# One core, two layers with 16 experts: weights rotate through eight places, four experts a loop round

## What is computed

```python
aff = softmax(h @ w_router)                 # (tokens, 16)
gsel, idx = top_k(aff.T, C)                 # every expert picks C tokens: 64 latent and 16 context
xs = h[idx]                                 # (16, C, 1024)
hid = silu(xs @ w_gate[e]) * (xs @ w_up[e]) # 1024 x 1024 weights, one set for each expert
ye = (hid @ w_down[e]) * gsel
x = x + g2 * scatter_add(ye, idx)
```

## Time and profile before

| what | value |
|---|---|
| device time, median of 3 runs | 1809.16 us (1808.12 to 1811.6) |
| span of the profiled execution | 1807.7 us |
| PE busy | 1619.1 us (90%) |
| DVE, ACT, POOL busy | 829.0, 572.2, 391.3 us |
| DMA traffic | 502.59 MB, mean 278 GB/s |
| expert stages | about 420 to 900 us and 1302 to 1782 us |

### The profile page before, as it was taken

The page is one execution under the profiler, slowest core; times in us unless marked ns, Lnnn a source line. Parts: engine busy times, 40 slices in busy tenths (PEclk is TensorE's granted clock), DMA queues, the critical chain, the costliest instruction groups (busy, mean ns, idle before and its releaser), DMA issues. The chain is left out here.

```text
span 1807.7 us, 69734 instructions
## 1 busy us (share of the span) xinstructions
PE 1619.1 (90%) x27905; PEld 1281.1 (71%) x27905; DVE 829.0 (46%) x2593; ACT 572.2 (32%) x2228; POOL 391.3 (22%) x2166
## 2 busy tenths in 40 slices
PE   6999988986999999888869999899599998998885
PEld 3554457446999989888735554664389988998885
DVE  2299768262333323232245996943623232423233
ACT  2200245235545432211130003542355554221211
POOL 1100000002343424332310000000124333333332
PEclk9999999997999999999989999999799999999998
DMA  9356640237999999999953412221599999999992
GB/s 348 129 184 235 233 174 1 105 127 284 402 409 409 409 409 409 409 409 409 361 206 140 157 58 102 108 94 35 202 374 409 409 409 409 408 409 409 409 407 111
DMA packets 146722, 502.59 MB, mean 278 GB/s; under 512 B 6217, under 2 KB 6642, under 8 KB 146578
## 3 DMA queue, kind: packets, MB, share of 16 engines
q1 hardware_dynamic: 142288, 488.96, 69.5%
q0 software_dynamic: 3264, 10.88, 1.8%
q10 hardware_dynamic: 1026, 1.25, 0.2%
HBM read 494.76 MB, written 6.31 MB: 277 GB/s over the span
## 5 line engine op out<-in xcount | busy, mean ns | idle before, releaser
L950 PE MATMUL ps<-v_sb,weight_ring 128*64 128x80 f32 x16384 | 589.3, 234 | 51.7 <-DMA weight_ring<-in_w_gate_dram 20.8
L950 PEld LDWEIGHTS ps<-v_sb,weight_ring 128*64 128x64 f32 x16384 | 577.3, 138 | 63.0 <-DMA weight_ring<-in_w_gate_dram 25.0
L967 PE MATMUL ps<-v_sb,weight_ring 128*64 128x80 f32 x8192 | 296.7, 234 | 31.7 <-DVE v_sb L1693 19.9
L967 PEld LDWEIGHTS ps<-v_sb,weight_ring 128*64 128x64 f32 x8192 | 288.4, 138 | 40.0 <-DVE v_sb L1693 25.0
L705 PE MATMUL ps<-mix,weight_ring 128*128 128x128 f32 (+1 forms) x976 | 271.0, 439 | 2.1 <-ACT mix L1054 1.2
L1238 ACT ACTIVATE v_sb<-mix 128x8 f32 x1520 | 185.5, 205 | 223.6 <-PE ps L950 146.1
L1719 DVE TENSOR_TENSOR qk<-qk,v_sb 128x8 f32 x1520 | 212.3, 194 | 90.8 <-issue 90.0
L1848 POOL COPY v_sb<-mix 128x8 f32 x1040 | 145.2, 198 | 479.0 <-PE ps L950 417.7
L1861 POOL TENSOR_TENSOR qk<-qk,v_sb 128x8 f32 x1040 | 198.7, 232 | 181.7 <-DVE v_sb L1708 178.5
L705 PEld LDWEIGHTS ps<-mix,weight_ring 128*128 128x128 f32 x976 | 148.1, 194 | 122.8 <-issue 119.8
L1443 DVE SCALAR_TENSOR_TENSOR weight_ring<-u_gate,conv_cols,weight_ring 128x655 f32<-128x655 f32 x240 | 195.3, 899 | 0.0
(11 more groups left out here) (195 smaller groups left out, 1240.5 us busy)
## 6 DMA issues: line engine op xcount, KB each, us to landing
weight_ring<-in_w_down_dram SPq DMA_DIRECT2D x64, 2048.0 KB, 23.7
weight_ring<-in_w_gate_dram SPq DMA_DIRECT2D x48, 2048.0 KB, 20.9
weight_ring<-in_w_up_dram SPq DMA_DIRECT2D x48, 2048.0 KB, 23.6
weight_ring<-in_w_mod_dram SPq DMA_DIRECT2D x24, 2048.0 KB, 9.0
weight_ring<-in_w_in_dram SPq DMA_DIRECT2D x10, 2048.0 KB, 8.3
spare<-in_w_gate_dram SPq DMA_DIRECT2D x32, 512.0 KB, 10.4
weight_ring<-in_w_out_dram SPq DMA_DIRECT2D x4, 2048.0 KB, 9.4
rope_sb<-in_w_gate_dram SPq DMA_DIRECT2D x16, 512.0 KB, 11.3
```

What stands on the lines that cost most here:

```text
L950: last = nc.tensor.matmul(ps[c * HALF:(c + 1) * HALF, 2 * (i % 2) + f // BLK, f % BLK * CAP:(f % BLK + 1) * CAP], w[:, kk, o:o + HALF], pi ...
L967: last = nc.tensor.matmul(ps[c * HALF:(c + 1) * HALF, 4 + d // BLK, d % BLK * CAP:(d % BLK + 1) * CAP], w[:, kk, o:o + HALF], hid[:, k, :] ...
```

## The change

Units are numbered n = 0 to 95 over a layer, and unit n lies in place n mod 8. Places 0 to 5 are the ring, places 6 and 7 the eight pieces that were the relays, now called `annex`; TensorE reads its weights there directly, and ScalarE's copies are gone. As 8 places and 6 units an expert repeat after 24 units, TensorE's loop has four experts a round and four rounds. The row of the final norm goes to `past_k_t` and is loaded in layer 1's attention. The index registers of the adds are read ahead of the wait for the result: the first group of each expert, all groups of the last. Core of the diff:

```diff
+UNITS = 6
+PIECES = KD // 2
+PLACES = SLOTS + 2
+ROUND = 4
...
+        def unit_rows(l, q, j):
+            if q < SLOTS:
+                return ring[:, UNIT_SLOTS[l][q], j * D:(j + 1) * D]
+            return annex[q - SLOTS][j]
+
+        def freed(slot):
+            return UNITS * EXPERTS - PLACES + UNIT_SLOTS[0].index(slot) + 1
...
+            def expert_unit(l, n):
+                src, q = expert_src(l, n // UNITS, n % UNITS), n % PLACES
+                if q < SLOTS:
+                    sp.dma_start(ring[:, UNIT_SLOTS[l][q], :]..., src).then_inc(expert_loaded[q].sem, 16)
+                    return
+                for j in range(PIECES):
+                    sp.dma_start(annex[q - SLOTS][j], src[:, j, :]).then_inc(expert_loaded[q].sem, 16)
...
-                        sp.wait_ge(*expert_used.at(l - 1, 6 * (EXPERTS - 1) + i + 1))
+                        sp.wait_ge(*expert_used.at(l - 1, freed(PROJ_SLOTS[l][i])))
...
-                for u in range(2, first if l > 0 else 0):
-                    sp.wait_ge(*expert_used.at(l - 1, 6 * (EXPERTS - 1) + 3 + u))
+                for u in range(first if l > 0 else 0):
+                    sp.wait_ge(*expert_used.at(l - 1, freed(mod_slot(l, u))))
                     mod_unit(l, u)
...
-                for e in range(1, EXPERTS):
-                    refill_relays(e + 1)
-                    for i in range(RELAYS if e < RELAY_END else 0, 6):
-                        sp.wait_ge(*expert_used.at(l, e * 6 + (i - 5)))
-                        expert_unit(l, e, i)
+                for n in range(PLACES, UNITS * EXPERTS):
+                    sp.wait_ge(*expert_used.at(l, n - PLACES + 1))
+                    expert_unit(l, n)
...
-                with nc.Fori(0, EXPERTS, engines=[mybir.EngineType.PE], hint_back_edge=True) as e:
-                    gate_up(e)
-                    pe.wait_ge(*result_taken.at(l, e + 1))
-                    down(e)
+                with nc.Fori(0, EXPERTS // ROUND, engines=[mybir.EngineType.PE], hint_back_edge=True) as g:
+                    for j in range(ROUND):
+                        gate_up(g, j)
+                        down(g, j)
...
-                    if e + 1 < RELAY_END:
-                        for r in range(RELAYS):
-                            relay_copy(e + 1, r)
...
+                    starts = range(0, add_split(e), PICK_LOAD)
+                    ahead = len(starts) if e + 1 == EXPERTS else 1
+                    loaded = [picks_of(mybir.EngineType.Pool, e, at, PICK_LOAD) for at in starts[:ahead]]
+                    pool.wait_ge(*result_taken.at(l, e + 2))
...
-                    pool.wait_ge(*expert_loaded[0].at(l - 1, RELAY_END))
+                    pool.wait_ge(*expert_used.at(l - 1, UNITS * EXPERTS))
...
+                if l + 1 == DEPTH:
+                    pool.wait_ge(*scores_done.at(l, ATT))
+                    pool.dma_start(final_gain, final_norm_g...).then_inc(gain_loaded.sem, 16)
...
-            pool.wait_ge(*expert_loaded[1].at(DEPTH - 1, RELAY_END))
-            pool.dma_start(x_norm[:], final_norm_g...).then_inc(gain_loaded.sem, 16)
```

More of the change, by code:

```diff
@@ L218, in build @@
         out_loaded = [signal(f"out_loaded{b}", 1, 16) for b in range(2)]
-        expert_loaded = [signal(f"expert_loaded{i}", EXPERTS, 16) for i in range(6)]
+        expert_loaded = [signal(f"expert_loaded{q}", UNITS * EXPERTS // PLACES, 16 if q < SLOTS else 16 * PIECES)
+                         for q in range(PLACES)]
         expert_used = signal("expert_used", 6 * EXPERTS)
-        relay_loaded = [signal(f"relay_loaded{r}", RELAY * (RELAY_END - 1), 16) for r in range(RELAYS)]
-        relay_copied = [signal(f"relay_copied{r}", (RELAY - 1) * (RELAY_END - 1)) for r in range(RELAYS)]
         rope_loaded = signal("rope_loaded", unit=16)
@@ L445, in _ @@
                 first, units = MOD_EARLY[l], len(MOD_LIST[l])
-                for u in range(2):
-                    if l > 0:
-                        sp.wait_ge(*expert_used.at(l - 1, 6 * (EXPERTS - 1) + 3 + u))
+                for u in range(2 if l == 0 else 0):
                     mod_unit(l, u)
@@ L495, in _ @@
                         sp.wait_ge(*out_done.at(l, TILES))
-                    expert_unit(l, 0, i)
-                for r in range(RELAYS):
-                    if r == 1:
+                    expert_unit(l, i)
+                for n in range(SLOTS, PLACES):
+                    if n == SLOTS + 1:
                         sp.wait_ge(*x2_ready.at(l, TILES))
@@ L502, in _ @@
                         sp.wait_ge(*x2_transposed.at(l, TILES - 1))
-                    for j in range(RELAY):
-                        relay_piece(l, 1, r, j)
+                    expert_unit(l, n)
                 sp.wait_ge(*top_round.at(l, TOP_ROUNDS))
@@ L1712, in add_hi @@
                 def add_hi(e):
-                    for at in range(add_split(e), CAP, PICK_LOAD):
-                        rows = picks_of(mybir.EngineType.DVE, e, at, PICK_LOAD)
-                        if at == add_split(e):
-                            dve.wait_ge(*result_taken.at(l, e + 2))
+                    starts = range(add_split(e), CAP, PICK_LOAD)
+                    ahead = len(starts) if e + 1 == EXPERTS else 1
+                    loaded = [picks_of(mybir.EngineType.DVE, e, at, PICK_LOAD) for at in starts[:ahead]]
+                    dve.wait_ge(*result_taken.at(l, e + 2))
+                    for g, at in enumerate(starts):
+                        rows = loaded[g] if g < ahead else picks_of(mybir.EngineType.DVE, e, at, PICK_LOAD)
                         for j, pick in enumerate(rows, at):
@@ L1851, in add_lo @@
                 def add_lo(e):
-                    for at in range(0, add_split(e), PICK_LOAD):
-                        rows = picks_of(mybir.EngineType.Pool, e, at, PICK_LOAD)
-                        if at == 0:
-                            pool.wait_ge(*result_taken.at(l, e + 2))
-                            if e > 0:
-                                pool.wait_ge(*added_lo.at(l, e))
-                                pool.wait_ge(*added_hi.at(l, e))
+                    starts = range(0, add_split(e), PICK_LOAD)
+                    ahead = len(starts) if e + 1 == EXPERTS else 1
+                    loaded = [picks_of(mybir.EngineType.Pool, e, at, PICK_LOAD) for at in starts[:ahead]]
+                    pool.wait_ge(*result_taken.at(l, e + 2))
+                    if e > 0:
+                        pool.wait_ge(*added_lo.at(l, e))
+                        pool.wait_ge(*added_hi.at(l, e))
+                    for g, at in enumerate(starts):
+                        rows = loaded[g] if g < ahead else picks_of(mybir.EngineType.Pool, e, at, PICK_LOAD)
                         for j, pick in enumerate(rows, at):
```

56 lines of the change are left out of this document (23 added, 33 removed).

## The result

The changed kernel takes 2014.8 us (median of 4 runs, 2008.05 to 2021.04), the kernel before, on the same chip, 1808.64 us. The ratio is 1.114, 95% interval 1.1118 to 1.1161: slower by 206 us. The forecast was 1922, the upper end of its range 2055.

What follows compares the result with a forecast made beforehand. Expert stages were held bound by the weight stream near 409 GB/s once TensorE used up its head start. Stage cost 118 - 2.0 - 1.65 = +114 on 1809 gave 1922 us, range 1800 to 2055.

Steps and rivals of the forecast that it cites:

- The round is refetched: TensorE's expert loop: the four-expert body of 24 instruction packets doesn't stay in memory, so each round fetches all 24 again.
- P = 5.5 us a packet: Expert stages: pace of one fetched packet of 128 matmuls, taken as 5.5 us between bounds 5.12 and 6.79.
- The branch back, 2.5 us: TensorE's loop end: jump to a packet no longer there, 2.5 us each, three times a stage, bounds 0 to 6.8.
- Sum for the stages: Each expert stage: 528 + 2.3 + 7.5 = 538 us against 479.3, a cost of 59 a layer, 118 in all.
- The range: Whole time if fetch sets the pace: 1850 us with 5.2 us a packet to 2055 with 6.2.
- Head start worth nothing, few waits for weights, DMA under 409 GB/s: Expert stages: eight preloaded units gain nothing, TensorE seldom waits for weights, and DMA runs below 409 GB/s.
- Places and first loads: Expert stages: eight places read directly gain 0 if fetch is the bound, up to 3.2 us a layer if the stream is.
- Index registers: Last expert's adds: POOL's index loads read ahead save 4 x 0.25 = 1.0 us a layer, 2 in all.
- Final norm row: Program's end: with the norm row loaded early, VectorE starts the last norm 1.65 us sooner.
- Rival 1: TensorE's loop: instruction fetch is hidden or the round is retained; 1799 to 1809 us, say 1804; 18% faster, 5% no change.
- Rival 2: Expert stages: one DMA engine carries all TensorE packets, so units land every 6.1 us; +117 a layer, 2040 us; chance 15%.

Runs made afterwards that it cites:

- experiment 3: Kernel before with one expert a pass, loop head at slot 0 and 96 or 160 tiny unused matmuls added to each pass: 2360.5 and 3129.11 us.
- Experiment 5: Changed kernel with both TensorE loop heads put at instruction slot 0, 80 or 160: 1941.52, 1992.75 and 2088.65 us.
- experiment 1: Kernel before with only TensorE's loop changed to four experts a round, relays and ScalarE copies kept: 2002.18 us, ratio 1.1087.
- experiment 4: Changed kernel, but from unit 8 of each layer on only a quarter of each unit's weights is loaded: 1752.31 us, ratio 0.9703.

## Why the prediction was right, and where it was short

The forecast's direction and mechanism hold; its +114 was +206. Step by step:

- **The round is refetched** (24 packets, four times): right. q8 has 226 packets against the 200 named: 38 + 36 distinct, 2 x 3 x 24 = 144 again, and about one more for each of the six branches back. But the argument that chose this from the rows does not hold: stalls at each new packet were to show that there is no room for 24. The kernel before stalls in that way although its six packets fit a memory that keeps eight (experiment 3), so such stalls say nothing of the size. Here the rows left the choice open, and it came out right by more than they showed.
- **P = 5.5 us a packet**: the mis-sized term. The rounds of layer 0 start at 420.51, 560.73, 700.52 and 839.50; one takes 139.7 us, of which 6.3 are the branch back, so 24 packets take 5.56 each. In layer 1 they start at 1376.78, 1530.86, 1687.74 and 1844.23: 155.8 us, less 3.4, makes 6.35. Both are within the bounds 5.12 to 6.79. The argument for the low value was that full places shorten the queues, from 6.28 down towards 4.8. They did: a gate unit's time to landing fell from 20.9 to 9.5 us (page, median). But that brought P to 5.56 only where the edge is at a unit's end. Rows that hinted at it stood there: layer 1's edge fell after 439 = 3 x 128 + 55 matmuls and its packets took 6.17 and 6.79 us; layer 0's fell after 509 = 3 x 128 + 125 and took 6.42 and 5.76. I averaged the four; two a layer would not have settled it. Experiment 5 shows the dependence. With both heads at slot 0, where both edges are at a unit's end, the stages are 548.2 and 540.6 us against the 538 of the forecast: the price was right for that place of the edge, and the place was in no term.
- **The branch back, 2.5 us**: it is 6.3 in layer 0 (the fourth expert of a round takes 39.7, 39.2 and 40.5 us, the others some 33.5) and 3.4 in layer 1 (41.5 against 38.1). The gap itself is 3.8 to 5.5 us, in the upper half of the bounds 0 to 6.8, and the fall of the clock behind it was in no term.
- **Sum for the stages**: 59 a layer was forecast, 76 and 135 measured. The 93 us that the forecast was short by are these 17 and 76: in layer 0 mostly the branch back (3 x 3.8 = 11), in layer 1 mostly P (90 packets x 0.85 = 77).
- **The range**: its lower end, 1850 with P = 5.2, leaves out the branch back; with the 2.5 us of the forecast it is 1865. The upper end, 2055, has it.
- **Head start worth nothing, few waits for weights, DMA under 409 GB/s**: right.
- **Places and first loads (0 in the sum, -3.2 a layer if the stream stayed the bound)**: right. No row shows a gain, since TensorE waits for its instructions; experiment 1 leaves the whole rest of the change between nothing and a loss.
- **Index registers (-2.0)**: wrong, 0. The step took POOL's loads for the path and the wait on `result_taken` for a long one; on VectorE there is none.
- **Final norm row (-1.65)**: -1.3 at the program's end by the traces, and not seen in the times. VectorE starts on time (12.0 us after the start of the last product, as forecast), but the granted clock, 0.50 since the idle time before the transposes, rises 14.4 us after that product with the row alone and 12.7 us after it before.
- **Rival 1** (hidden or retained) fell. The Trainium skill ("Runtime: NRT & Kernel Launch", section "Instruction fetch mechanics") says that fetch is hidden, as the sequencer dispatches more slowly than the memory is filled; this case agrees only where there is no full stream beside it (experiment 4, and the last expert of layer 1), and disagrees with 225 us of issue waits where there is. **Rival 2** gave 2040, nearer to the measured time than the forecast, but for another reason: it wanted landings to be waited for, and there is no such wait. A near number was no proof of it.

Of the kernels that compute everything, none beats the one before; the early row and the index registers are as fast as it.

## What to carry to other kernels

Count a loop body in instructions before unrolling it. On TensorE a body of up to eight packets of 256 was fetched once; bodies of 9, 12 and 24 packets were fetched whole in every pass, and beside a full weight stream a packet then took 5.5 to 6.4 us where it is executed in 4.5. If such a loop is unavoidable, try where its head lies: here packet edges just ahead of the release of a buffer gave 73 us over where they had fallen. And look which engine makes the value that an instruction waits for before moving loads ahead of the wait.

## What the runs showed of the hardware that was not expected

- A loop over the edge of the memory by a single packet keeps nothing: q8 43 against 317 (experiment 3).
- The place of a packet's edge within a unit of 128 matmuls changes a stage from 548 to 626 us in layer 0 and from 541 to 616 in layer 1, with the same instructions and bytes. A fetch of 16 KB is moved in 1.0 us in all of them; what changes is how long it waits before.
- 1920 empty instructions of VectorE a layer, 40% busy as it is, add 16.6 us to a stream that has nothing to do with it, 1.1 us for a packet of 8 KB that is itself moved in 0.32 us.
- An idle time of 4.4 us at a branch back leaves TensorE at a granted clock of 0.50 for some 5 us of work in layer 0 (700.52 to 705.25).
